# A second Strassen block per gate-up pair, with the weight sums in a buffer of their own

## The reference

```
x = x + HybridMixer(RMSNorm(x))                 # RG-LRU branch and attention branch, merged
x = x + CrossAttention(RMSNorm(x), RMSNorm(mem))
h = RMSNorm(x)
x = x + (silu(h @ w_gate) * (h @ w_up)) @ w_down    # w_gate, w_up: 2048 x 5632, w_down: 5632 x 2048
return RMSNorm(x)
```

## Time and profile before

| | |
|---|---|
| median of 3 runs | 1775.4 us (1774.69 to 1776.0) |
| the profiled execution's own time | 1774.84 us |
| its span, first to last instruction | 1772.7 us |
| PE / DVE / ACT busy, share of the span | 99% / 65% / 52% |
| loads by SP into `w_raw` | q1, 327.72 MB |

### The profile page before, as it was taken

The page is one execution under the profiler, slowest core; times in us unless marked ns, Lnnn a source line. Parts: engine busy times, 40 slices in busy tenths (PEclk is TensorE's granted clock), DMA queues, the critical chain, the costliest instruction groups (busy, mean ns, idle before and its releaser), DMA issues.

```text
span 1772.7 us, 20039 instructions
## 1 busy us (share of the span) xinstructions
PE 1756.4 (99%) x8001; PEld 1459.6 (82%) x8001; DVE 1144.1 (65%) x1217; ACT 927.4 (52%) x1147; POOL 27.1 (2%) x51
## 2 busy tenths in 40 slices
PE   9999999999999999999999999999999999999998
PEld 7888888888888888888888888888888888888876
DVE  7577677655455454555665576777777677777774
ACT  6767668444545544544455454555444444554453
POOL 1000000000000000000000000000000000000000
PEclk9999999999999999999999999999999999999999
DMA  8565665666575756566755455666666566666564
GB/s 281 176 202 166 194 202 187 204 194 174 177 212 158 217 162 189 173 190 208 247 184 186 155 168 167 190 195 194 191 193 210 171 203 195 193 192 194 183 215 141
DMA packets 175757, 338.22 MB, mean 191 GB/s; under 512 B 10672, under 2 KB 15280, under 8 KB 175152
## 3 DMA queue, kind: packets, MB, share of 16 engines
q1 hardware_dynamic: 173232, 327.72, 60.3%
q0 software_dynamic: 1008, 5.24, 0.9%
q10 hardware_dynamic: 1424, 3.97, 0.6%
HBM read 334.80 MB, written 2.10 MB: 190 GB/s over the span
## 4 chain that ended last, share of the span: by engine, by line
PE 94%; DMA 3%; DVE 2%; ACT 1%; issue 0%; ACTq 0%; POOLq 0%; POOL 0%; DVEq 0%
PE group L429 29%; PE group L431 29%; PE group L430 29%; DMA w_raw<-in_w_ffn_down 2%; PE side L489 2%; DVE w_lo L1100 1%; PE side L431 1%; PE side L430 1%; PE side L429 1%; ACT w_hi L745 0%; DMA x_T_in<-in_x_T 0%; PE side L590 0%; PE side L574 0%; PE group L717 0%; PE group L716 0%
## 5 line engine op out<-in xcount | busy, mean ns | idle before, releaser
L1100 DVE TENSOR_TENSOR w_lo<-w_raw,w_hi 128x1024 fp32r<-128x1024 f32 (+1 forms) x646 | 776.5, 1209 | 542.8 <-ACT w_hi L745 536.4
L745 ACT ACTIVATE w_hi<-w_raw 128x1024 fp32r<-128x1024 f32 (+1 forms) x646 | 674.0, 1048 | 763.6 <-PE group L431 663.0
L429 PE MATMUL group<-w_hi,x_hi 128*128 128x512 f32 x1568 | 614.1, 392 | 0.3 <-DVE w_lo L1173 0.3
L431 PE MATMUL group<-w_hi,x_lo 128*128 128x512 f32 x1568 | 610.5, 389 | 0.0
L430 PE MATMUL group<-w_lo,x_hi 128*128 128x512 f32 x1568 | 610.2, 389 | 0.0
L431 PEld LDWEIGHTS group<-w_hi,x_lo 128*128 128x128 f32 x1568 | 294.3, 188 | 61.1
L429 PEld LDWEIGHTS group<-w_hi,x_hi 128*128 128x128 f32 x1568 | 294.5, 188 | 60.5 <-issue 0.7
L430 PEld LDWEIGHTS group<-w_lo,x_hi 128*128 128x128 f32 x1568 | 294.5, 188 | 59.8
L429 PE MATMUL group<-w_hi,v_hi 128*128 128x512 f32 x320 | 125.2, 391 | 0.0
L431 PE MATMUL group<-w_hi,v_lo 128*128 128x512 f32 x320 | 124.6, 389 | 0.0
L430 PE MATMUL group<-w_lo,v_hi 128*128 128x512 f32 x320 | 124.5, 389 | 0.0
(11 more groups left out here) (306 smaller groups left out, 1338.9 us busy)
## 6 DMA issues: line engine op xcount, KB each, us to landing
w_raw<-in_w_in SPq DMA_DIRECT2D x223, 512.0 KB, 4.1
w_raw<-in_w_ffn_gate SPq DMA_DIRECT2D x88, 512.0 KB, 4.3
w_raw<-in_w_ffn_up SPq DMA_DIRECT2D x88, 512.0 KB, 4.3
w_raw<-in_w_ffn_down SPq DMA_DIRECT2D x88, 512.0 KB, 4.9
w_raw<-in_w_rnn_proj SPq DMA_DIRECT2D x32, 512.0 KB, 4.8
w_raw<-in_w_attn_proj SPq DMA_DIRECT2D x32, 512.0 KB, 3.8
w_raw<-in_w_mix_out SPq DMA_DIRECT2D x32, 512.0 KB, 4.5
w_raw<-in_w_xkv SPq DMA_DIRECT2D x16, 512.0 KB, 3.8
```

The lines of the kernel that those rows point to most:

```text
L429: nc.tensor.matmul(out, h, whi[:, s, k, :], start=start, stop=False)
L431: return nc.tensor.matmul(out, l, whi[:, s, k, :], start=False, stop=stop)
L745: nc.scalar.activation(whi[:, s, ks], raw[:, s, ks], ACT.Copy).then_inc(hi_ready[s], 1)
L1100: V_.tensor_tensor(wlo[:, s, ks], raw[:, s, ks], whi[:, s, ks].bitcast(F32), ALU.subtract).then_inc(w_ready[s], 1)
```

## The change

The plan of ten of the eleven gate-up pairs (all but `gate_a` 0) has a second W, for row group 5, in place of the O for it, and the W for row group 3 comes earlier:

```diff
-UP_PLAN = "O0 O1 O2 O4 W3 O5 O6 O7".split()
+UP_PLAN = "O0 O1 W3 O2 O4 W5 O6 O7".split()
```

The sums for C and D go to a new buffer `w_sums` (8 KB per partition, over the region of `gain_final`), and the ring of raw slots counts loads only:

```diff
+LOADED = [_n for _n in range(CHUNKS) if KIND.get(_n) not in ("C", "D")]
+LOAD_OF = {_n: _load for _load, _n in enumerate(LOADED)}
...
+        def raw_of(n):
+            return LOAD_OF[n] % R, LOAD_OF[n] // R
...
             def load(n, w, row, col):
-                s, before = slot_of(n)
-                sync.wait_ge(w_ready[s], START + before)
+                s, _ = raw_of(n)
+                if LOAD_OF[n] >= R:
+                    earlier, used = slot_of(LOADED[LOAD_OF[n] - R])
+                    sync.wait_ge(w_ready[earlier], START + used + 1)
...
             def weight_sums(m):
...
-                T1_T3 = tiles[:, 2 * c:2 * c + 3:2, :]
-                then(V_.tensor_tensor(T1_T3, tiles[:, a:a + 4:3, :], tiles[:, a + 2:a + 3, :].to_broadcast([P, 2, GW]), ALU.add))
-                then(V_.tensor_tensor(raw[:, d, 1], raw[:, c, 0], tiles[:, a + 3, :], ALU.add))
-                dve.sem_inc(raw_full[d], 16)
-                V_.tensor_tensor(raw[:, c, 1], raw[:, d, 1], tiles[:, a + 1, :], ALU.add).then_inc(raw_full[c], 16)
+                a = 2 * raw_of(m)[0]
+                then(V_.tensor_tensor(w_sums[:, :, 0, :], tiles[:, a:a + 4:3, :], tiles[:, a + 2:a + 3, :].to_broadcast([P, 2, GW]), ALU.add))
+                then(V_.tensor_tensor(w_sums[:, 1, 1, :], w_sums[:, 0, 0, :], tiles[:, a + 3, :], ALU.add))
+                dve.sem_inc(sem("sum_D"), 1)
+                V_.tensor_tensor(w_sums[:, 0, 1, :], w_sums[:, 1, 1, :], tiles[:, a + 1, :], ALU.add).then_inc(sem("sum_C"), 1)
```

```diff
-            pool.dma_start(gain_final[:, :], ...)            # after the norm of mem
...
+            pool.wait_ge(sem("folded"), sum(last_sum(first) is not None for first in STEPS))
+            pool.dma_start(gain_final[:, :], ...)            # after the last pair's fold
```

More of the change, by code:

```diff
@@ L209, in build @@
         stage = [at(f"stage{n}", STAGE[n], [TT, GW]) for n in range(2)]
+        silu = stage[0]
         LW = region(8 * K1)
@@ L249, in build @@
         side = [ctx.enter_context(nc.psum_tensor(f"side{p}", [P, NB, SEQ], F32)) for p in range(2)]
-        P1, Q5, P7, P6 = [side[i // 2][:, 2 * (i % 2):2 * (i % 2) + 2, :].rearrange("p a b -> p (a b)") for i in range(4)]
+        P7, P6, P1, Q5 = [side[i // 2][:, 2 * (i % 2):2 * (i % 2) + 2, :].rearrange("p a b -> p (a b)") for i in range(4)]
         raw_full = [sem(f"raw_full{s}") for s in range(R)]
@@ L673, in _ @@
                             res_T("x2", GI["cross_out", KG - 1], KG - 1)
-                        if c == 4 and j > 0:
+                        if c == 3 and j > 0:
                             inners += 1
@@ L680, in _ @@
                             pe.wait_ge(sem("sums_lo"), 1)
-                            if inners:
-                                pe.wait_ge(sem("inner_lo"), inners)
                             if folds:
                                 pe.wait_ge(sem("folded"), folds)
+                        if kind == "D" and kp == FIRST_SUM[first] and inners:
+                            pe.wait_ge(sem("inner_lo"), inners)
                     if last_sum(first) is not None:
@@ L689, in _ @@
                     for c, kind, kp in pair_of(("down_" + part, q), inner_hi, inner_lo, fs_hi, fs_lo, F_SUMS[part]):
-                        if c == 4 and q == 0:
+                        if c == 3 and q == 0:
                             inners += 1
@@ L741, in splits @@
                         s, used = slot_of(m)
+                        if m in LOAD_OF:
+                            r, turn = raw_of(m)
+                            src = raw[:, r]
+                            act.wait_ge(raw_full[r], 16 * (turn + 1))
+                        else:
+                            src = w_sums[:, "CD".index(KIND[m])]
+                            act.wait_ge(sem("sum_" + KIND[m]), SUM_OF[m])
                         ks = slice(1, 2) if KIND.get(m) == "B" else slice(0, CK)
-                        act.wait_ge(raw_full[s], 16 * (used + 1))
                         act.wait_ge(w_used[s], START + used)
-                        nc.scalar.activation(whi[:, s, ks], raw[:, s, ks], ACT.Copy).then_inc(hi_ready[s], 1)
+                        nc.scalar.activation(whi[:, s, ks], src[:, ks], ACT.Copy).then_inc(hi_ready[s], 1)
             def evac(g, end, dst, scale, func):
@@ L1050, in _ @@
                                 gate_tanh(("gate_" + part, j - 1))
[L1051 removed]
+                            if c == 3:
                                 inner_split((j - 1) * NB, summed)
[L1053 removed]
+                            if c == 5 and summed:
                                 sums_hi(fs_hi[:, F_SUMS[part].index(2 * (j - 1))], f_sum[:, :, :])
```

43 lines of the change are left out of this document (23 added, 20 removed).

## The result

The median went from 1775.68 us (4 runs) to 1763.39 us (1763.25 to 1764.45, 4 runs): a ratio of 0.9931, 95% interval [0.9918, 0.9943], faster by 12.3 us. The profiled execution has a span of 1761.4 us.

The account below looks back on a forecast made before the run. PE, busy 99%, was taken as the bound, plus the few places where it waits. 1774.84 - 6.8 (matmuls) - 5.4 (ring) + 0.5 (new waits) = 1763.1 us, or 1763.7 against the median; range 1762.0 to 1769.0.

Parts of the forecast that it names:

- The matmuls: In ten pairs one O entry (24 matmuls) becomes one W entry (21): 30 matmuls fewer on PE, 6.8 us saved.
- The ring: Down pairs: loads issued earlier remove PE's five waits for `w_lo`, 5.7 us; 5.4 taken, bounds 0 and 5.7.
- The new waits: Behind the first block, five pairs with token sums: PE waits 0 to 0.3 us, 0.1 taken each, 0.5 together.
- The second block's slack: A of the second block, chunks 12 to 15: slack 1.0 us with token sums, 2.2 without; priced at nothing.
- The landings: Load of B of the second block: 4.7 us taken, as two loads are issued close together; median 4.3, slowest 6.2.
- The joins and the gain: Joins at a pair's end and the final gain's load of 7.2 us make PE wait for nothing: priced at nothing.
- Small new waits in all ten pairs: Rival: remainder behind D or A of second block late by 0.2 to 0.5 us, 1766 to 1769 us; 15%.
- The ring giving little: Rival: bunched loads merely queue behind each other, so the down pairs keep their waits, 1769.1 us; 7%.
- The slower one: Rival: second block's B load late in ten pairs; beyond 1.6 us mean slack, each us costs 10 us; 4%.

Follow-up runs that it names:

- the run of the ring alone: Changed kernel with the old plan for the gate-up pairs (one W, at row group 3): 1769.57 us, 0.9966 against before.
- the run with the old ring: Changed kernel with loads waiting as before the change and the sums for C and D in `w_raw`: 1781.48 us, 1.0033 against before.
- the kernel with the third block: Changed kernel with token sums one step later, a third block in `down_a` 0 and `inner_lo` awaited at the first D: 1763.41 us, then 1761.68 us.

## Why the prediction was right

It said 1763.7 us, the median is 1763.39; the point is how its steps fared. That the two agree to 0.3 us is in part luck, since two terms were off in opposite directions and the start of the program varies by more.

*The matmuls.* 30 x 0.227 = 6.8 us. Plan against no plan, the SwiGLU part differs by 719.0 - 713.2 = 5.8; with the new delays of 1.2 put back that is 7.0, of which 0.3 are starts that lie a little further apart behind the transposes in the run of the ring alone. Right, as the pair of 43.06 instead of 43.74 us shows most directly. By the figure of 131 ns of the Trainium skill (TensorE: Matmul & The Clock Gate, "Back-to-back issue gap") it would have been 3.9; the run of the ring alone speaks for the row.

*The ring.* 5.7 us of waits were to go, 5.4 was taken. At the five places the starts of PE's timeline lie 5.8 us too far apart before, with the matmuls just behind them, and all of it is gone; the run of the ring alone gave 724.6 - 719.0 = 5.6. The 0.3 that was set aside for `down_a` 2 came as a restart of 0.17 there. Right, and that the waits came from the ring's rule is shown by the run with the old ring, where they are back.

*The new waits.* 0.1 us in five pairs was taken, bounds 0 to 0.3; it is 0.2 in just these five, and moving the token sums removes them. With the restarts at A of two second blocks it makes 1.2 us where 0.5 was taken. The miss is that a remainder which arrives just in time still costs a restart.

*The second block's slack.* 1.0 and 2.2 us were worked out. The timeline has 0.1 to 1.1 (mean 0.75) with token sums and 1.5 to 1.9 (mean 1.8) without: right in order, a little too large in both. The landing taken, 4.7, is what the ten loads of B took (4.65 on the mean). What was too early is their issue. With token sums the remainder of chunk 9 was to end 1.2 us after D; in `gate_a` 2 it ends at 1146.48 + 1.23 = 1147.71, 1.7 us after, held up by ACT's `w_hi`. In `gate_a` 4 a landing of 5.2 took nearly all of the slack, so this step held with less room than it claimed.

*The landings.* The Trainium skill (DMA: Bandwidth & Descriptors, "Latency and other measured facts") gives 0.2 us for access to HBM on average and 2 us at high load, from which the prediction read longer landings for bunched loads. The trace agrees in direction. B's load took 4.65 us on the mean and 3.9 when it was issued later, and in the down pairs the loads of B of W4, issued in a bunch, took 6.1 (`down_a` 0) and 6.5 us (`down_a` 2). That the access to HBM is the reason no run here shows.

*The joins and the gain.* Nothing was priced, and PE waits for neither. The joins have cover only with the ring of loads: with the old one they became a wait.

*Sum.* 6.8 + 5.8 - 1.2 = 11.4, as measured in the SwiGLU part, where the prediction has 6.8 + 5.4 - 0.5 = 11.7. The medians differ by 12.3; the first 1048 us vary by up to 2 us between executions and can account for the rest, which is not shown, as only one execution before the change was profiled.

*The rivals.* Small new waits in all ten pairs: only five, too small to count. The ring giving little: refuted in the time, though its premise has something in it, since the bunched loads of `down_a` 0 and 2 land no sooner than the 5.73 us before; they are issued early enough all the same. The slower one, through B's load: the place is right (a PE wait at A of the second block when the load is late), and so is the price of one microsecond per pair for each microsecond of arrival beyond the slack. But the mean slack of 1.6 hid that the pairs with token sums pay from 0.75 on: at 1.3 and 0.2 us of later arrival, on the mean under 1.6, the time already rose by 3.4 us.

What the prediction didn't name is that the parts of the change hang together. It added two gains, but without the ring the plan is a loss (1781.48), and without the early product of silu as well (1780.05).

## What to carry to other kernels

When DVE writes into slots of a ring that a DMA queue fills, the queue's look-ahead shrinks by those slots just where the consumers are fastest; a small buffer for the computed tiles gives it back, and before adding work that consumes faster, that look-ahead is to be had first. To judge a denser plan, write down for each chunk when its producer can finish and when PE needs it, with the distances between starts from the timeline: slacks of 1 us decided everything here, while the busy shares (67% DVE) said nothing. Read such a slack in every repetition and not in one: in five like pairs it was 0.1 to 1.1 us. And when a delay is put in on purpose, measure the arrival too: loads issued 2.3 us later arrived only 1.4 us later. And where a kernel's start varies by more than the effect, compare the stretch that the change touches.

## What the runs showed of the hardware

The program's start has two forms. In the kernel with the third block, run twice, the windows from 8 to 12 and from 12 to 16 us read (busy PE, PEld, DVE, ACT, POOL, granted clock, DMA share, GB/s), first run then second:

```profile
8.00:12.00 4.00, 2.51 (x11) 1.38 (x9) 2.86 (x6) 3.29 (x7) 0.00 (x0) 1.00 1.05 398
12.00:16.00 4.00, 3.28 (x8) 2.66 (x9) 4.00 (x7) 4.00 (x8) 0.00 (x0) 0.59 0.98 339
```

```profile
8.00:12.00 4.00, 3.64 (x11) 2.54 (x9) 2.77 (x5) 3.10 (x7) 0.00 (x0) 1.00 1.05 399
12.00:16.00 4.00, 3.35 (x15) 2.81 (x16) 4.00 (x7) 4.00 (x8) 0.00 (x0) 1.00 1.01 355
```

In the first run PE is busy for only 2.51 of 4 us, and in the next stretch the granted clock is 0.59: part of it at the lower of its two levels, 1.2 GHz. In the second PE is busy for 3.64 of 4 us and the clock stays at 2.4 GHz. The last transposes of `x_res` start at 1049.9 and 1048.2, and over all twelve profiles they start at 1047.9 to 1048.5 in the six where the clock stayed and at 1049.4 to 1050.2 in the six where it fell: 1 to 2 us that no edit here made, for one and the same kernel lay once on this side and once on that. What lies ahead of the fall is one wait of PE for the remainder of one of the first chunks, 1.0 us or less where the clock stayed and 2.0 to 3.0 in all six where it fell; why that wait is longer in some executions stays open.

The same happened behind four of the long waits of the kernel with three gate-up blocks; above, the starts 0.43 apart follow an idle time of 1.84 us. The windows at another of the four:

```profile
1608.00:1610.00 2.00, 0.64 (x3) 0.55 (x4) 2.00 (x4) 1.80 (x2) 0.00 (x0) 1.00 0.00 0
1610.00:1613.50 3.50, 3.50 (x10) 2.73 (x9) 2.71 (x3) 1.61 (x3) 0.00 (x0) 0.51 0.85 266
```

The granted clock is at 0.51, the lower level, after a stretch in which PE was busy for 0.64 of 2 us. So a wait of 1.77 to 1.84 us was followed four times by 1.6 us more (seven matmuls start 0.20 later each, and one on either side of them 0.14 and 0.06). It need not be: the other six long waits of that kernel (1.77 to 1.88) have no such rows behind them, and the run with the load delayed by two chunks has a wait of 2.06 us without them.
